# Six places for the weights of a three-block network: low parts in place, one high part ahead of each norm, parameters first, and the feed-forward's second unit behind its first

## What is computed

```python
for l in range(DEPTH):
    h = _rmsnorm(x, g_mix[l])
    proj = h @ w_in[l]
    ...
    branch = jnp.einsum('bsnc,ncd->bsnd', ys, w_branch[l])
    gates = jax.nn.sigmoid(gate_pre.reshape(bsz, seq, N_BRANCH, D_MODEL) + gate_b[l])
    mixed = jnp.sum(gates * branch, axis=2)
    x = x + mixed @ w_out[l]
    x = x + _conv_ffn(_rmsnorm(x, g_ffn[l]), w_up[l], ffn_conv_w[l], ffn_conv_b[l], w_down[l])
```

## Time and profile before

| | us |
|---|---|
| median of 3 runs | 1458.65 |
| the profiled execution, its own time | 1458.64 |
| its span on the core | 1456.9 |
| PE busy | 1428.7 (98%) |
| POOL busy | 1184.2 (81%) |
| ACT busy | 883.8 (61%) |
| DVE busy | 709.3 (49%) |

### The profile page before, as it was taken

One profiled execution on the slowest core, in us unless ns is written; L12 is line 12 of the kernel. 1 busy time (PEld: TensorE's weight loads), 2 busy tenths in 40 slices (PEclk: granted clock), 3 DMA queues, 4 the chain that ended last, 5 costly groups with the idle time before them and its releaser, 6 DMA issues.

```text
span 1456.9 us, 29053 instructions
## 1 busy us (share of the span) xinstructions
PE 1428.7 (98%) x9384; PEld 1292.4 (89%) x9384; DVE 709.3 (49%) x1605; ACT 883.8 (61%) x1499; POOL 1184.2 (81%) x926
## 2 busy tenths in 40 slices
PE   8999999999999999999999999999999999999998
PEld 7899998888878899987888889999899999888887
DVE  3653444555555733355545556670563542444444
ACT  5665645766666655647666666866445544755554
POOL 5877687999978776787999969899676799799985
PEclk9999999999999999999999999999999999999999
DMA  7654455666656554455665666556444465566662
GB/s 251 196 156 149 144 160 151 195 191 189 191 170 194 170 157 137 154 176 156 199 190 189 187 194 192 161 174 192 139 132 130 148 194 180 165 196 188 188 191 96
DMA packets 80037, 251.80 MB, mean 173 GB/s; under 512 B 7633, under 2 KB 22481, under 8 KB 79441
## 3 DMA queue, kind: packets, MB, share of 16 engines
q1 hardware_dynamic: 79088, 245.72, 54.6%
q10 hardware_dynamic: 864, 4.92, 1.0%
HBM read 249.56 MB, written 1.05 MB: 172 GB/s over the span
## 4 chain that ended last, share of the span: by engine, by line
PE 92%; ACT 3%; DVE 2%; issue 2%; DMA 0%; POOL 0%; SPq 0%; ACTq 0%; DVEq 0%; POOLq 0%
PE psum L959 21%; PE psum L960 20%; PE psum L961 20%; PE psum L991 16%; PE psum L993 8%; PE psum L1070 1%; PE psum L1136 1%; PE psum L1089 1%; ACT w_hi L436 1%; PE psum L1080 1%; PE psum L1058 0%; DMA raw<-in_units 0%; PE psum L1137 0%; PE psum L1097 0%; PE psum L1403 0%
## 5 line engine op out<-in xcount | busy, mean ns | idle before, releaser
L411 POOL TENSOR_TENSOR w_lo<-raw,w_hi 128x512 fp32r<-128x512 f32 x461 | 601.4, 1305 | 256.0 <-ACT w_hi L436 246.2
L412 POOL TENSOR_TENSOR w_lo<-raw,w_hi 128x512 fp32r<-128x512 f32 x461 | 608.2, 1319 | 0.0
L436 ACT ACTIVATE w_hi<-raw 128x1024 fp32r<-128x1024 f32 x461 | 486.0, 1056 | 187.7 <-PE psum L993 94.7
L959 PE MATMUL psum<-both,w_hi 128*128 128x256 f32 x1192 | 346.1, 290 | 2.3 <-POOL w_lo L412 2.3
L960 PE MATMUL psum<-both,w_lo 128*128 128x256 f32 x1192 | 337.5, 283 | 0.0
L961 PE MATMUL psum<-both,w_hi 128*128 128x256 f32 x1192 | 337.5, 283 | 0.0
L991 PE MATMUL psum<-both,w_hi 128*128 128x512 f32 x1040 | 259.3, 391 | 5.5 <-DVEq L1590 5.5
L959 PEld LDWEIGHTS psum<-both,w_hi 128*128 128x128 f32 x1192 | 228.7, 192 | 11.8 <-issue 8.5
L960 PEld LDWEIGHTS psum<-both,w_lo 128*128 128x128 f32 x1192 | 228.9, 192 | 0.3
L961 PEld LDWEIGHTS psum<-both,w_hi 128*128 128x128 f32 x1192 | 228.8, 192 | 0.0
L991 PEld LDWEIGHTS psum<-both,w_hi 128*128 128x128 f32 x1040 | 190.7, 188 | 42.6 <-POOL w_lo L412 4.6
(11 more groups left out here) (301 smaller groups left out, 2199.9 us busy)
## 6 DMA issues: line engine op xcount, KB each, us to landing
raw<-in_units SPq DMA_DIRECT2D x461, 512.0 KB, 3.5
arena<-in_consts ACTq DMA_DIRECT2D x1, 2320.0 KB, 9.0
arena<-in_bias ACTq DMA_DIRECT2D x2, 1024.0 KB, 4.8
arena<-in_consts SPq DMA_DIRECT2D x1, 1657.0 KB, 8.3
out<-arena SPq DMA_DIRECT2D x4, 256.0 KB, 2.7
pre<-in_x SPq DMA_DIRECT2D x2, 256.0 KB, 3.4
arena<-in_x SPq DMA_DIRECT2D x2, 256.0 KB, 4.7
prm<-in_params ACTq DMA_DIRECT2D x2, 153.5 KB, 2.6
```

What stands on the lines that cost most here:

```text
L411: pool.tensor_tensor(w_lo[s][:, 0:D // 2], raw[s][:, 0:D // 2], w_hi[s][:, 0:D // 2].bitcast(F32), ALU.subtract)
L412: pool.tensor_tensor(w_lo[s][:, D // 2:D], raw[s][:, D // 2:D], w_hi[s][:, D // 2:D].bitcast(F32), ALU.subtract)\
L436: act.activation(w_hi[s][:, :], raw[s][:, :], ACT.Copy).then_inc(hi_ready, d.inc(hi_ready))
L959: pe.matmul(out, hi, r_hi, start=start, stop=False, **kw)
```

## The change

- **Places.** `W_RING` = 6 places. `raw` and `w_lo` now lie at the same addresses (the `landing` stack gives its space back before `w_lo` is allotted), so the low part overwrites the raw unit. The space is the same: 6 x 2 tiles instead of 4 x 3.
- **Waits.** The load of unit u+6 waits for `unit_done` of unit u, and for nothing else. `high()` waits for the load alone, POOL for `hi_ready` alone.
- **High parts.** Layer 0's norm has one `high()` more, behind its squares (`beside=1`). From there on each `high()` works on a unit one later than before. Ahead of each other norm there is one `high()` more at its start, and one fewer behind it: `late_norm` sets `early[0] = 1`, so that the next call, in `ffn_act`, does nothing.
- **Parameters.** Layer 0's parameters are asked for before all else on ACT's queue. The constants of the first block are loaded without their first three parts, after the loads of units 0 to 7.
- **Feed-forward.** PE runs the eight pieces for the first unit alone; the second is an ordinary `up_unit()` behind it, ahead of the factors.
- Three loops are written out (`gated_branch` on ACT and PE, the retention's units on PE), since six places don't divide them.

```diff
-        raw = [sb(f"raw{s}", D) for s in range(RING)]
-        w_hi = [sb(f"w_hi{s}", D, F32R) for s in range(RING)]
-        w_lo = [sb(f"w_lo{s}", D, F32R) for s in range(RING)]
+        raw = []
+        with ExitStack() as landing:
+            for s in range(W_RING):
+                raw.append(landing.enter_context(nc.sbuf_tensor(f"raw{s}", [P, D], F32)))
+        w_lo = [sb(f"w_lo{s}", D, F32R) for s in range(W_RING)]
+        w_hi = [sb(f"w_hi{s}", D, F32R) for s in range(W_RING)]
...
+            def landing_free(u):
+
+                if u is None or u >= W_RING:
+                    sp.wait_ge(unit_done, d.next(unit_done))
...
-            def load(index, s):
-
-                sp.wait_ge(hi_ready, d.next(hi_ready))
-                sp.wait_ge(lo_ready, d.next(lo_ready))
+            def load(index, s, u=None):
+                landing_free(u)
...
             def low(s):
-                pool.wait_ge(raw_full[s], d.next(raw_full[s]))
                 pool.wait_ge(hi_ready, d.next(hi_ready))
-                pool.wait_ge(unit_done, d.next(unit_done, 1, "slot"))
...
             def high(n=1):
 
                 for _ in range(n):
+                    if early[0]:
+                        early[0] -= 1
+                        continue
...
                     act.wait_ge(raw_full[s], d.next(raw_full[s]))
-                    act.wait_ge(unit_done, d.next(unit_done, 1, "slot"))
...
-            def norm(load, gain, ahead=0, new_params=False):
+            def norm(load, gain, ahead=0, new_params=False, beside=0):
                 root_mean_square(load)
+                high(beside)
...
             def late_norm(gain, spare):
 
+                high()
                 act.activation(small[:, 57:58], small[:, 60:61], ACT.Sqrt)
...
                 high()
+                early[0] = 1
...
-                pair = []
-                for _ in range(2):
-                    pair.append((unit(), next_slot()))
-                    pe.wait_ge(slot_free, d.next(slot_free))
+                s, k = unit(), next_slot()
+                pe.wait_ge(slot_free, d.next(slot_free))
...
+                up_unit()
                 pe.wait_ge(root_rows, d.next(root_rows))
```

More of the change, by code:

```diff
@@ L377, in _ @@
                     else:
-                        load(at + order[u], s)
+                        load(at + order[k], u % W_RING, u)
                 first, end = layer * UNITS1 + len(order), (layer + 1) * UNITS1
[L380 to L383, removed]
+                groups = (end - first) // W_RING
                 with d.loop(groups) as i:
-                    for s in range(RING):
-                        load(i * RING + (first + ahead + s + layer * PAD1), s)
@@ L387, in _ @@
-                for u in range(first + ahead + groups * RING, end):
-                    load(u + layer * PAD1, u % RING)
-            with d.loop((total_units - REAL) // RING) as i:
-                for s in range(RING):
-                    load(i * RING + (REAL + s + DEPTH * PAD1), s)
-            for u in range(total_units - total_units % RING, total_units):
-                load(u + DEPTH * PAD1, u % RING)
+                    for k in range(W_RING):
+                        load(i * W_RING + (first + k + layer * PAD1), (first + k) % W_RING)
@@ L395, in _ @@
+                for u in range(first + groups * W_RING, end):
+                    load(u + layer * PAD1, u % W_RING)
+            groups = (total_units - REAL) // W_RING
+            with d.loop(groups) as i:
+                for k in range(W_RING):
+                    load(i * W_RING + (REAL + k + DEPTH * PAD1), (REAL + k) % W_RING)
+            for u in range(REAL + groups * W_RING, total_units):
+                load(u + DEPTH * PAD1, u % W_RING)
             for b in range(4):
@@ L820, in gated_branch @@
             def gated_branch():
[L821 to L826 removed]
+                for c in range(CH):
+                    act.activation(chunk(pre, c % 2), slot(take()), ACT.Sigmoid).then_inc(act_out, d.inc(act_out))
+                    high()
+                    d.skip(unit_done)
+                    next_slot()
             for c in range(CH + 2):
@@ L1305, in _ @@
                 linear_unit(h_hi, h_lo)
-            def linear_units(n, src_hi=h_hi, src_lo=h_lo):
-                with d.loop(n // RING) as _:
-                    for _ in range(RING):
-                        linear_unit(src_hi, src_lo)
             def turn_rows(at):
@@ L1496, in _ @@
                     last.then_inc(rbc_ready, d.inc(rbc_ready))
-            with d.loop(3) as _:
-                for _ in range(2):
-                    linear_unit(h_hi, h_lo)
-                    linear_unit(y1_hi, y1_lo)
+            for _ in range(CH - 2):
+                linear_unit(h_hi, h_lo)
+                linear_unit(y1_hi, y1_lo)
             gated_branch()
```

75 lines of the change are left out of this document (34 added, 41 removed).

## The result

After the change the kernel takes 1471.81 us (median of 4 runs, 1469.74 to 1473.62), before it 1458.93 us beside it: ratio 1.0093, 95% interval 1.008 to 1.0106. The forecast was 1465.2 with a range up to 1471.0. The direction was right, the size was not: +12.9 us instead of +6.5, outside the range. The profiled execution took 1473.62 us by its own time, span 1471.8, so it is 15.0 us behind that of before (1458.64).

The account below looks back on a forecast made before the run. PE was busy for 98% of the span, leaving some 28 us idle and lower-clock stretches to win. Start -3.4, entries +7.8, exits +1.6, elsewhere +0.5 summed to +6.5 us: 1465.2 us, range 1456.5 to 1471.

Parts of the forecast that it names:

- Start: Block 0's start: PE's wait of 2.27 us and the low clock behind it go, less 0.35 us for parameters; -3.4 us.
- Elsewhere: Attention and the rest: a few high parts ahead of a wait of PE may come 0.3 us late; +0.5 us.
- What the new waits make of a `high()`: ACT, all along: each high part waits for a load behind the unit six back; 0.7 to 0.8 us later in feed-forwards.
- smallest rival: Start not won: raws 6 and 7 land late behind the bias, sigmoids hold up the next units; 1468.5 us, chance 0.05.
- Entries: Entry to each of three feed-forwards: the third high part's load holds up squares and pieces; +2.6 us each, +7.8 in all.
- ACT on time: Rival: loads early enough that no high part holds up ACT, entries 0.6 us, exits nothing; 1457.5 us, chance 0.13.
- Exits: Exit from a feed-forward, twice: the last tile's high part and its chain come 0.8 us later; +1.6 us.
- the clock one: Rival: longer PE idling at entries and exits makes the clock fall more often, +3 to +6 us; some 1469 us, chance 0.14.
- The rule that was set aside: Repeated gaps can mean too little SBUF; by it the 4.0 us of PE's waits for POOL would go in full.

Follow-up runs that it names:

- e_nobeside: The changed kernel without the high part beside the root in block 0, so each later high part is made one unit later; 1456.31 us.
- l_four_ahead: The changed kernel with two high parts behind block 0's pieces instead of three, so four are made ahead instead of five; 1453.22 us.
- h_before_start: The kernel before with the start of the change alone: block 0's parameters first, unit 1's high part beside the root; 1455.35 us.
- d_biaslate: The changed kernel with the load of the 1 MB bias issued behind the first two sigmoids instead of ahead of them; 1471.03 us.
- b_pair: The changed kernel with the two first up units of each feed-forward interleaved over the pieces again; 1482.88 us.
- k_pair_head_start: b_pair with four high parts ahead instead of five (beside the root one, behind block 0's pieces two); 1448.28 us.
- i_old_order: The changed kernel without the high parts beside block 0's root and ahead of the feed-forwards' roots, the first two up units interleaved; 1455.14 us.

## Why the prediction was off, by its own steps

The mechanism was right, and so was the direction. Two terms of the sum failed: the start, where the mechanism wasn't applied, and "Elsewhere", which put the clock's falls at nothing.

**What the new waits make of a `high()`: right, and it is the cause.** "At each point of ACT's program `high()` now works on a unit one later than before": e_nobeside and l_four_ahead take that away and 15.5 and 18.6 us go. The prediction said so, but priced it at the entries and exits of the feed-forwards alone.

**Start: a step that failed.** Forecast -3.4, measured -0.75 (201.87 to 201.12), and -2.1 to -2.6 in the four other traces with the same start (199.24 to 199.80). The wait at 22 and the clock behind it went as worked out (h_before_start shows the full gain), but a wait of 2.88 us (1.23 to 1.75 in the four) took their place. The prediction had this as its smallest rival, 0.05, in the words "raws 6 and 7 land late behind the bias, and the sigmoids hold up the next units". d_biaslate shows that it is the bias, and l_four_ahead that it needs the fifth high part too. Missed by 2.7 us in this execution, by 0.8 to 1.3 in the others; why the same wait differs so was not tried. The rule was in the text; it was applied to the feed-forwards and not to the start, where the two loads share DMA with the bias and the constants.

**Elsewhere: the other step that failed, 0.5 forecast, 4.0 measured.** 2.7 of it is the stretch behind layer 0's exit (4.95 to 7.68), all clock: two half-clock stretches behind a wait of 3.05 us where before, after 1.99 us, there was none. The sum had no term for the clock here; it stood only among the rivals. 0.8 is the new wait at 457, where layer 1's sigmoids meet the bias again.

**Entries: right; the sum 1.2 us short through the clock.** Forecast 3 x 2.6 = 7.8, measured 2.78 + 3.10 + 3.16 = 9.0. The pieces are 1.8 to 2.1 us late (PE's idle time is 2.27 to 2.59 instead of 0.49), and 0.95 us comes back at the factors (1.21 for 2.15). d_biaslate has an entry without a fall of the clock at +2.5; the falls add 0.3 to 0.7 each. With ACT on time the forecast was +0.6; l_four_ahead has +0.55 and +0.57. What the second unit's place costs depends on the count: with five ahead it is a gain (b_pair), with four it costs 1.5 to 1.6 us an entry (57.19 us in l_four_ahead and 55.62 in k_pair_head_start for the first).

**Exits: 0.8 was 1.0 and 1.7 us.** In layer 0 the wait grew from 1.99 to 3.05 us, in layer 1 to 3.65. Forecast 1.6, measured 2.7. The high part came 1.1 us behind the up unit's end, not 0.8; the load takes 3.7 us in the median and not 3.5.

The terms missed: 2.7 + 1.2 + 1.1 + 3.5 = 8.5, which is 15.0 - 6.5. The median, 1471.81, is 6.6 us above the forecast; by the four other starts about 1 us of the miss recurs at the start, and the rest of the 2.7 belongs to this execution.

The rivals: the clock one was right as a mechanism (four more half-clock stretches) and in its size. The falls that the sum left out cost 1.6 us at the entries and 2.7 at the exit, 4.3 in all, where the prediction had 3 to 6. The prediction had the rivals as alternatives, though each follows from the same cause, ACT being late, and both came. By the prediction a fall followed one in two of such stretches; the trace of before has five stretches of 1.99 us and more, and two falls. The Trainium skill's TensorE: Matmul & The Clock Gate (Why this matters for your kernels), which warns of idle gaps between bursts, bears on this rival; but its warning is of longer gaps than the 2.5 and 2.8 us that were forecast, so that by it the rival was not the likeliest case, although the prediction says so. Here the clock also fell behind gaps of 2.27, 2.39 and 2.59 us. The rule that was set aside, the Trainium skill's Perfetto Trace Analysis (Optimization Strategy), that a repeated gap can mean too little SBUF, would have had the 4.0 us of waits for POOL go; in i_old_order, with six places and the old order, they are 4.0 us still.

Open: why the same wait at an exit is 3.05 us in layer 0 and 3.65 in layer 1 of the changed kernel, and 3.54 and 3.71 without the early high part, was not tried. And d_biaslate's second half-clock stretch at 1256 was not settled: the clock's falls differ from run to run, and the profiled execution of the changed kernel (1473.62, granted clock 0.993 in the mean) is the slowest of four that go down to 1469.74 (0.995).

## What to carry to other kernels

In a chain of load, convert and use over a ring of places, the number made ahead has an upper bound as well as a lower one: here 3, 4 and 5 ahead of 6 places gave 1459, 1448 and 1483 us with all else equal. When an in-place ring ties the load's start to the end of a use, count how many uses lie between the issue of a load and the instruction that waits for its landing. Hold their time against the landing, with the shortest use and beside the largest other transfer. And do not judge edits one by one while such a count is wrong: the sign of the pair's order turned with it. Rivals that share a cause can all come true at once: add their costs.

## What the runs showed of the hardware

The clock's fall to 1.2 GHz in or behind an idle stretch of PE, over all fourteen traces of this case, from the first 5 us on: of 54 waits of 0.9 to 1.8 us none came with one; of 4 waits of 1.99 us one; of 26 from 2.15 to 2.9 us twelve; of 14 from 3.05 to 3.92 us all. The same wait (2.15 us behind the factors) came with a fall in h_before_start at 254 and not at 672, in i_old_order at 672 and not at 257. Each of these falls lasted 3.4 us at 1.2 GHz, or twice that.

What a fall costs depends on the place. Behind an exit, up to the wait for rows, one cost 1.6 us (6.53 in layer 1 of before, 4.95 without) and two 2.7 (7.68). At the start one cost 1.4: from PE's wait for rows near 14 to the y_hi wait it is 187.39 us in before, with a fall behind the wait of 2.27 us, and 185.95 in i_old_order, with the same wait and no fall. Behind the pieces of a feed-forward, where PE waits for ACT anyway, a fall cost 0.3 to 0.7.
